# Spreading the running sums of dt times a over 128 partitions: a DRAM round trip by DMA in place of 32 one-hot matmuls

## The reference, cut to what matters

```python
dt = jax.nn.softplus(dt_raw.astype(jnp.float32) + dt_bias.astype(jnp.float32))
a = -jnp.exp(a_log.astype(jnp.float32))
...
x = (xh * dt[..., None]).reshape(bsz, nc, L, g, r, hd)
a_dt = jnp.moveaxis((dt * a.astype(f32)).reshape(bsz, nc, L, g, r), 2, -1)
a_cs = jnp.cumsum(a_dt, axis=-1)
causal = jnp.tril(jnp.ones((L, L), dtype=bool))
decay = jnp.exp(jnp.where(causal, a_cs[..., :, None] - a_cs[..., None, :], -jnp.inf))
cb = jnp.einsum("bclgn,bcsgn->bcgls", cc, bc)
scores = cb[:, :, :, None] * decay
y_diag = jnp.einsum("bcgrls,bcsgrp->bclgrp", scores, x)
```

## Time and profile before

| | |
|---|---|
| runs of the kernel | 2731.21 us median of 3 (2731.16 to 2733.67) |
| the profiled execution | 2730.92 us, its span 2729.1 us |
| PE, PEld busy | 2663.7 us (98%), 2285.8 us (84%) |
| DVE, ACT, POOL busy | 1923.1 us (70%), 1495.9 us (55%), 391.2 us (14%) |
| granted clock of PE | 0.994 of full speed |
| DMA | 486.55 MB, mean 178 GB/s; queue q1 busy 57.9% of 16 engines' span |

### The profile page before, as it was taken

One profiled execution on the slowest core, in us unless ns is written; L12 is line 12 of the kernel. 1 busy time (PEld: TensorE's weight loads), 2 busy tenths in 40 slices (PEclk: granted clock), 3 DMA queues, 4 the chain that ended last, 5 costly groups with the idle time before them and its releaser, 6 DMA issues.

```text
span 2729.1 us, 38657 instructions
## 1 busy us (share of the span) xinstructions
PE 2663.7 (98%) x15042; PEld 2285.8 (84%) x15042; DVE 1923.1 (70%) x2916; ACT 1495.9 (55%) x2307; POOL 391.2 (14%) x391
## 2 busy tenths in 40 slices
PE   7999999999998999999999999999999999999997
PEld 7888888888886888888888887878888888888886
DVE  8777776676787665656565679677877676776775
ACT  6555566767555444444444456535565555555554
POOL 3011100312511001010101034020201010101012
PEclk9999999999999999999999999999999999999999
DMA  7555565555564555666666656545666666666663
GB/s 245 171 185 182 181 196 171 154 171 155 158 184 139 174 159 166 186 189 185 186 185 187 188 164 199 175 124 174 189 187 191 189 190 189 191 191 189 190 180 122
DMA packets 133487, 486.55 MB, mean 178 GB/s; under 512 B 14935, under 2 KB 15224, under 8 KB 133304
## 3 DMA queue, kind: packets, MB, share of 16 engines
q1 hardware_dynamic: 133304, 484.08, 57.9%
HBM read 481.92 MB, written 2.10 MB: 177 GB/s over the span
## 4 chain that ended last, share of the span: by engine, by line
PE 88%; DVE 8%; ACT 2%; issue 2%; DMA 0%; DVEq 0%; ACTq 0%; SPq 0%
PE ps L690 56%; PE ps L691 28%; DVE wl L1190 3%; ACT wh L908 1%; DVE hT L1190 1%; DVE X L1196 1%; PE ps L779 1%; PE ps L844 0%; PE ps L877 0%; DVE A L1196 0%; DVE R L1190 0%; DVE T L1196 0%; DVE Gf L1190 0%; DVE T L1190 0%; PE ps L790 0%
## 5 line engine op out<-in xcount | busy, mean ns | idle before, releaser
L690 PE MATMUL ps<-X,wh 128*128 128x512 f32 x4848 | 1713.8, 399 | 3.7 <-DVE hT L1190 2.1
L1190 DVE TENSOR_TENSOR wl<-raw,wh 128x1024 fp32r<-128x1024 f32 x902 | 1139.1, 1267 | 732.1 <-ACT wh L908 731.3
L908 ACT ACTIVATE wh<-raw 128x1024 fp32r<-128x1024 f32 x902 | 952.3, 1059 | 971.0 <-PE ps L691 950.9
L691 PE MATMUL ps<-X,wl 128*128 128x256 f32 x4848 | 1354.0, 279 | 0.0
L690 PEld LDWEIGHTS ps<-X,wh 128*128 128x128 f32 x4848 | 910.3, 188 | 232.1 <-issue 9.5
L691 PEld LDWEIGHTS ps<-X,wl 128*128 128x128 f32 x4848 | 914.1, 189 | 3.6 <-issue 1.9
L690 PE MATMUL ps<-XG,wh 128*128 128x512 f32 x2304 | 817.4, 399 | 30.7 <-DVE hT L1190 16.3
L691 PE MATMUL ps<-XG,wl 128*128 128x256 f32 x2304 | 644.7, 280 | 0.0
L690 PEld LDWEIGHTS ps<-XG,wh 128*128 128x128 f32 x2304 | 433.6, 188 | 144.3 <-DVE hT L1190 22.1
L691 PEld LDWEIGHTS ps<-XG,wl 128*128 128x128 f32 x2304 | 435.9, 189 | 0.9
L1645 POOL TENSOR_TENSOR hT<-hT,T 128x256 f32<-128x256 f32 x224 | 184.9, 848 | 1466.5 <-DVE hT L1190 1466.5
(11 more groups left out here) (170 smaller groups left out, 1132.8 us busy)
## 6 DMA issues: line engine op xcount, KB each, us to landing
raw<-in_w_gate SPq DMA_DIRECT2D x176, 512.0 KB, 3.6
raw<-in_w_down SPq DMA_DIRECT2D x176, 512.0 KB, 3.7
raw<-in_w_sc SPq DMA_DIRECT2D x96, 512.0 KB, 4.2
raw<-in_w_up SPq DMA_DIRECT2D x88, 512.0 KB, 3.6
raw<-in_w_val SPq DMA_DIRECT2D x88, 512.0 KB, 3.6
raw<-in_w_zx SPq DMA_DIRECT2D x80, 512.0 KB, 3.7
raw<-in_w_in SPq DMA_DIRECT2D x68, 512.0 KB, 3.7
raw<-in_w_osc SPq DMA_DIRECT2D x32, 512.0 KB, 3.6
```

The lines of the kernel that those rows point to most:

```text
L690: e.matmul(bank(c, i)[:, :], W1, x, start=st, stop=False)
L691: t = e.matmul(bank(c, i)[:, 0:256], W2, x[:, 0:256], start=False, stop=sp)
L908: return e.activation(out, in_, ACT.Copy, scale=scale)
L1190: return e.tensor_tensor(out, a, b, op)
```

## The change

The rows of `acs` are written once to a DRAM scratch tensor of 16 x 512 words (one row for each pair of heads). For each pair SP then issues a DMA that reads this 2 KB row for each of 128 partitions into one of three buffers `bb` of 512 words in SBUF, six steps before `ssd0`. The Relus read that buffer in place of the PSUM bank. The two matmuls of line 779, their semaphore and PE's waits for the bank go.

```diff
         if c.kind == "dt":
             for n in range(7):
                 put(e + 2 + n, "dt%d" % n, c)
+            put(e + 8, "acsw", 0)
...
                     SSD0[j] = b
+                    put(b - 6, "ssdl", j)
                     put(b, "ssd0", j)
...
+    bb = lambda q: a_(6400 + 512 * q, 512)
+    acs_dram = nc.dram_tensor("acs_rows", (16, 512), F32).ap()
...
+                if piece == "acsw":
+                    w.wait_ge(dtV, 13)
+                    e.dma_start(acs_dram.rearrange("j (h t) -> (j h) t", h=2), acs).then_inc(d_acs, 16)
+                if piece == "ssdl":
+                    w.wait_ge(d_acs, 16)
+                    if i > 2:
+                        w.wait_ge(sR, 4 * (i - 2))
+                    else:
+                        w.wait_ge(cb, 4)
+                    e.dma_start(bb(i % 3), acs_dram[i:i + 1, :].to_broadcast([128, 512])).then_inc(d_bb[i % 3], 16)
...
                 if piece == "ssd0":
-                    tb, bb = banks[4 + i % 2], banks[6 + i % 2]
+                    tb = banks[4 + i % 2]
                     w.wait_ge(xbc, 8 + i + 1)
                     if i > 1:
                         w.wait_ge(s4, i - 1)
-                        w.wait_ge(sR, 4 * (i - 1))
...
                     t.then_inc(sT, 1)
-                    w.wait_ge(dtV, 13)
-                    if i % 2 == 0 and sn_n:
-                        w.wait_ge(snv, 5 * (sn_n - 1) + 1)
-                    for hh in range(2):
-                        t = e.matmul(bb[:, 256 * hh:256 * hh + 256], ident[0:32, 2 * i + hh:2 * i + hh + 1].to_broadcast([32, 128]),
-                                     acs, start=True, stop=True)
-                    t.then_inc(sB, 1)
...
                 if piece == "sn0":
                     w.wait_ge(s6, 3 * i + 3)
-                    w.wait_ge(sR, 4 * (bb_n - (bb_n + 1) % 2))
+                    if i:
+                        w.wait_ge(snv, 5 * (i - 1) + 1)
...
                 if piece == "ssd1":
-                    w.wait_ge(sB, i + 1)
+                    w.wait_ge(d_bb[i % 3], 16 * (i // 3 + 1))
...
-                            e.activation(o, banks[6 + q][:, 256 * hh + 128 * st:256 * hh + 256], ACT.Relu, scale=-1.0,
+                            e.activation(o, bb(i % 3)[:, 256 * hh + 128 * st:256 * hh + 256], ACT.Relu, scale=-1.0,
                                          bias=dcol[:, c0:c0 + 1]).then_inc(sR, 1)
```

More of the change, by code:

```diff
@@ L446, in program @@
     dtA, dtV, dtP, xbc, cb, cbv, zs = (sem(n) for n in ("dtA", "dtV", "dtP", "xbc", "cb", "cbv", "zs"))
-    sT, sB, sx, sR, sE, sMg, sMv, sY, s4, s5, sS, s6 = (sem(n) for n in (
-        "sT", "sB", "sx", "sR", "sE", "sMg", "sMv", "sY", "s4", "s5", "sS", "s6"))
+    d_acs, d_bb = sem("d_acs"), [sem(f"d_bb{i}") for i in range(3)]
+    sT, sx, sR, sE, sMg, sMv, sY, s4, s5, sS, s6 = (sem(n) for n in (
+        "sT", "sx", "sR", "sE", "sMg", "sMv", "sY", "s4", "s5", "sS", "s6"))
     snm, snA, snv, yv = (sem(n) for n in ("snm", "snA", "snv", "yv"))
@@ L663, in tensor @@
         w = Waits(e)
-        bb_n, sn_n = 0, 0
         def unit(u):
@@ L774, in tensor @@
                     t.then_inc(sT, 1)
-                    w.wait_ge(dtV, 13)
-                    if i % 2 == 0 and sn_n:
-                        w.wait_ge(snv, 5 * (sn_n - 1) + 1)
-                    for hh in range(2):
-                        t = e.matmul(bb[:, 256 * hh:256 * hh + 256], ident[0:32, 2 * i + hh:2 * i + hh + 1].to_broadcast([32, 128]),
-                                     acs, start=True, stop=True)
-                    t.then_inc(sB, 1)
-                    bb_n = i + 1
                 if piece == "ssd3":
@@ L795, in tensor @@
                     w.wait_ge(s6, 3 * i + 3)
-                    w.wait_ge(sR, 4 * (bb_n - (bb_n + 1) % 2))
+                    if i:
+                        w.wait_ge(snv, 5 * (i - 1) + 1)
                     e.matmul(banks[6][:, 0:256], ones[:, :], sacc(i), start=True, stop=True).then_inc(snm, 1)
-                    sn_n = i + 1
                 if piece == "att0":
```

## The result

The changed kernel takes 2718.09 us (median of 6 runs, 2712.86 to 2726.25); the kernel before, run beside it, 2733.99 us (6 runs, 2731.16 to 2735.42). That is 15.9 us less, a ratio of 0.9941 with a 95% interval of 0.9925 to 0.9957. The forecast was 2712 us, a gain of 19.1, with a range of 2707 to 2721.

A forecast was written before the change was run, and what follows sets the result against it. PE was taken to bound the kernel, busy 98% of the span. Savings of 5 x 1.17 + 11 x 1.20 = 19.1 us, all else hidden, took the median from 2731.2 to 2712.1 us; range 2707 to 2721.

The forecast's parts named there:

- 19.1 us from the removed matmuls and the switches around them: PE in the sixteen pairs: 1.17 us saved in each of five, 1.20 in each of eleven; ends 17.0 and 19.9.
- The rival in which the transposes stay as dear as now: PE's transposes before each unit take over the hidden time; gain 16 to 17.5 us, 2714.2 us; chance 0.12.
- All waits on SP already satisfied, the transfers hidden: SP and DMA queues: one 32 KB write and 16 loads of 256 KB cost nothing; weight loads have 5 us of room.
- The landing time: Broadcast load of a row: taken as 2.5 us, between 1.8 by bytes and 5.5 at worst, seven steps ahead of ACT's need.
- the rival of 2753 us: DMA queues: broadcast reads of 8 us delay weight loads and PE, 22 us slower; chance 0.06.
- ACT keeps up: ACT in the dearest pair: 12.07 us busy of 12.54, 0.47 to spare; Relus from SBUF at most 1.9 us more, hidden.
- PE still busy all the time from 440 us to the end of the pairs.: Sign expected in the profile after: PE without holes through the pairs, at 12.5 us from pair to pair.
- the rival in which ACT binds: ACT needs 0.5 us more than PE in eight pairs with other table loads; 4 us lost, 2716.1 us; chance 0.12.
- unchanged within a microsecond or two: Sign expected in the profile after: the time from the end of the pairs to the end of the span stays.
- a clock of 1.00 only in the pairs: Sign expected in the profile after: granted clock stays at 1.00 in the stretch of the pairs.

The follow-up runs named there:

- onehot128: The kernel before, with its one-hot matmuls over 128 rows instead of 32, padded with zeros: 2729.8 us, ratio 0.9978 to the kernel before.
- both_ways: The changed kernel with the 32 one-hot matmuls put back, DMAs still issued and waited for, Relus reading PSUM: 2735.35 us, ratio 0.9997 to the kernel before.
- three_loads: The changed kernel with only the first three broadcast loads, later pairs reading a wrong row: 2717.95 us, ratio 0.9936 to the kernel before.
- serial3: The changed kernel with each row loaded three times in series, so that SP is held: 2745.76 us, ratio 1.0041 to the kernel before.
- smooth: The changed kernel with a third PSUM bank for the transposes of x and the residual ahead of the mask product: 2716.62 us, ratio 0.9938.

## Why the prediction was right

*Forecast: 19.1 us from the removed matmuls and the switches around them.* Right, and by the mechanism given. The distances fell by 19.6 us: 0.19 us stays at a steady pair where I took 0.22, 0.13 at the others where I took 0.20. The rival in which the transposes stay as dear as now is refuted by both rows, and `onehot128` shows that the idle times belonged to the switch of shape. Of the 19.6 us the medians show 15.9, inside the range: 1.9 us went into new holes, 0.5 has no cause shown, and 1.3 were lost right behind the pairs. That this sum meets the median to a tenth is luck, since single times move by 12.7 us with PE's pace and by 5 with the clock.

*All waits on SP already satisfied, the transfers hidden.* Right: `both_ways` and `three_loads` price them at nothing, and `serial3` shows where the cover would have ended. The landing time was mis-sized: 4.0 us, not 2.5, for half the bytes of a weight load that lands after 3.7. The landing time alone could hide a read at half the rate, but the trace's packet records settle it: the 2 KB packets of these loads take 84 ns in the median and the 4 KB packets of the weight loads 159. At 8 packets for each of the 16 DMA engines that is 0.7 us of transfer in 4.0 us of landing. What fills the rest no run separates. Slow reads of one DRAM row by 128 partitions, the rival of 2753 us, did not happen. The Trainium skill, DMA: Bandwidth & Descriptors, section Latency and other measured facts, reports that copies between tensors with a row pitch of 4 or 8 MiB ran at half the rate. Rows at distance zero show no such fall in these runs.

*ACT keeps up.* Nearly right. The pair of the earlier trace rows takes 12.41 us with ACT busy 10.74, where I had 12.54 and 12.07; pair 1 takes 12.47 with 11.36. So ACT had more room than the sum gave it, and its waits for PE fell to 43 us, forecast 45. The Relus from SBUF take 495 and 388 ns where they took 474 and 368 from PSUM: 64 x 0.02 = 1.3 us, hidden.

*"PE still busy all the time from 440 us to the end of the pairs."* Wrong. Beside two group norms ACT and DVE are behind, and 1.9 us of the 19.6 go into new holes. That comes nearest to the rival in which ACT binds, at half the price that I gave it (4 us), but at the norms instead of the pairs with table loads, and with DVE as the one that PE waits for in both holes. `smooth` shows that they are no accident of one bank or of one order.

*The time after the pairs "unchanged within a microsecond or two".* Wrong for single executions: PE's pace moves it by up to 13 us, and the clock near 850 us by up to 5. I had bounded the range by the terms of the change; what made the profiled execution lose 12 us was in none of them. The part that does go with the change is within the microsecond or two: 1.3 us right behind the pairs, 0.3 for a longer hole and 1.0 for the fall of the clock behind it. The prediction asked for a clock of 1.00 only in the pairs, where it held, and did not ask what a longer hole would do to the clock behind them.

## What to carry to other kernels

Price a small matmul in a stream of large ones by the distance between starts around it, the idle time of the weight loads included: here the switch from 128 rows to 32 and back cost 0.38 us of the 1.25 us that each use of it took, and padding to 128 rows alone gave that back. Measure up to the second large matmul behind it: up to the first it looked like 0.47. A transfer on an in-order queue is free as long as its wait is already satisfied when the queue gets there, and as long as what stands behind has room; work out that room first (here 5 to 7 us, and the runs found it between 4.4 and 9). When two profiles of long kernels are compared, count the matmuls in a stretch in which nothing changed before a difference is given to the change.

## What the runs showed of the hardware

- PE's steady stream has two paces: 346.7 and 353.3 ns for a pair of a 512- and a 256-column matmul (1.9%), both at a granted clock of 1.00. An unbroken stretch keeps its pace; a break of a single transpose can change it, either way. In a stretch of 1910 pairs that is 12.7 us, and the times of one kernel fall into two clusters 13 us apart, in agreement with the pace of that stretch in the profiles. Where the breaks are the same, the order of paces was the same in two executions, but the stretch of 1910 pairs differs between executions of one kernel. What decides is open: a stretch of 1487 pairs was slow in all twelve profiles in which it was unbroken.
- A 32-row float32 matmul of 256 columns among 128-row ones took longer with its switches than the same over 128 rows: 1.75 us against 1.37 for two of them, from the first transpose to the second matmul of the next unit.
- 128 partitions reading the same 2 KB row of DRAM are not slow: 4.0 us to land in the median, 5.6 at most, and 84 ns a packet of 2 KB where a packet of 4 KB takes 159.
- Behind a hole of 1.80 to 1.82 us in PE's stream the granted clock fell from 2.4 to 1.2 GHz for some 3.4 us in eight profiles and stayed in one; behind holes of 1.48 to 1.71 us at the same place of the program it stayed in all five. It cost 0.8 to 1.1 us a time. What decides is open.
